# Two transformer blocks with 32 experts: expert rows gathered by products with a 0/1 matrix instead of a scatter, sorted rows and row copies

## What is computed

```
def hier_moe(h, P, l):
    t = h.reshape(-1, d)
    grp_prob = softmax(t @ P['moe_wg'][l] + P['moe_bg'][l])
    grp_gate, grp_idx = lax.top_k(grp_prob, 1)
    ...
    top_p, top_i = lax.top_k(softmax(sel), TOP_K_IN_GROUP)
    w = grp_gate * top_p / jnp.sum(top_p)
    def body(acc, xs):
        wg_e, wu_e, wd_e, cw = xs
        y = (silu(t @ wg_e) * (t @ wu_e)) @ wd_e
        return acc + cw[:, None] * y, None
```

## Time and profile before

| | us |
|---|---|
| median of three runs | 1150.37 |
| lowest and highest | 1147.16, 1150.96 |
| the profiled execution, its own time | 1151.86 |
| its span, first to last instruction | 1150.1 |
| PE busy / DVE busy / ACT busy / POOL busy | 970.8 / 487.3 / 332.5 / 138.0 |
| read from HBM | 291.87 MB |

### The profile page before, as it was taken

The page is one execution under the profiler, slowest core; times in us unless marked ns, Lnnn a source line. Parts: engine busy times, 40 slices in busy tenths (PEclk is TensorE's granted clock), DMA queues, the critical chain, the costliest instruction groups (busy, mean ns, idle before and its releaser), DMA issues.

```text
span 1150.1 us, 20717 instructions
## 1 busy us (share of the span) xinstructions
PE 970.8 (84%) x7674; PEld 646.0 (56%) x7674; DVE 487.3 (42%) x1271; ACT 332.5 (29%) x879; POOL 138.0 (12%) x193
## 2 busy tenths in 40 slices
PE   5899888999468788788879999998964887888887
PEld 3456655655345455455558888776543554555454
DVE  2079876521632333333430314685145332333334
ACT  3211353530522222221330101575132222222222
POOL 0400140000400010000010055000022100010000
PEclk8999999999679999988979999998976999999998
DMA  9999736772269999999873323100215799999993
GB/s 353 279 316 361 254 110 234 264 271 74 101 229 374 416 416 417 419 418 418 337 257 110 96 87 129 56 1 2 78 69 219 298 416 417 416 417 417 417 418 126
DMA packets 84913, 302.08 MB, mean 263 GB/s; under 512 B 5541, under 2 KB 34449, under 8 KB 68465
## 3 DMA queue, kind: packets, MB, share of 16 engines
q1 hardware_dynamic: 81584, 291.03, 65.4%
q0 software_dynamic: 2832, 8.61, 2.6%
q10 hardware_dynamic: 432, 1.57, 0.3%
HBM read 291.87 MB, written 9.32 MB: 262 GB/s over the span
## 4 chain that ended last, share of the span: by engine, by line
PE 51%; DMA 26%; DVE 14%; ACT 3%; issue 3%; SPq 1%; POOL 1%; POOLq 0%; DVEq 0%; ACTq 0%
PE banks L666 26%; DMA ring<-in_moe_w_up_dram 24%; PE banks L978 6%; PE banks L675 5%; DVE a L1508 5%; PE banks L1022 4%; PE banks L973 4%; DVE a L1443 2%; PE banks L704 2%; PE banks L1001 1%; DVE rt L1443 1%; SPq L561 1%; DMA bc<-in_moe_be_dram 1%; PE banks L949 1%; POOL bc L2041 1%
## 5 line engine op out<-in xcount | busy, mean ns | idle before, releaser
L666 PE MATMUL banks<-ring,hT 128*128 128x256 f32 (+1 forms) x720 | 153.9, 376 | 1.7 <-ACT hT L1164 1.6
L666 PEld LDWEIGHTS banks<-ring,hT 128*128 128x128 f32 x720 | 135.0, 191 | 21.3 <-DMA ring<-in_ev_w_in_dram 1.9
L1216 ACT ACTIVATE a<-banks 32x256 f32<-32x256 f32 (+1 forms) x208 | 88.3, 425 | 199.0 <-PE banks L1001 100.5
L1539 DVE SCALAR_TENSOR_TENSOR xT<-banks,mod,xT 128x128 f32<-128x128 f32 x352 | 118.7, 409 | 63.0 <-PE banks L1022 63.0
L1022 PE MATMUL banks<-a 128*128 128x384 f32 x352 | 134.0, 527 | 3.5 <-ACT a L1216 3.3
L1443 DVE TENSOR_TENSOR a<-a,banks 64x128 f32<-64x128 f32 (+1 forms) x64 | 21.7, 340 | 268.9 <-ACT a L1199 268.9
L666 PE MATMUL banks<-hT,ring 128*128 128x384 f32 x384 | 127.9, 493 | 1.6 <-ACT hT L1164 1.6
L978 PE MATMUL banks<-ring,a 128*32 128x128 f32 x2560 | 92.1, 304 | 43.1 <-DMA ring<-in_moe_w_up_dram 42.5
L978 PEld LDWEIGHTS banks<-ring,a 128*32 128x32 f32 x2560 | 80.5, 122 | 69.5 <-issue 68.4
L973 PE MATMUL banks<-ring,a 128*64 128x256 f32 x704 | 85.7, 398 | 25.5 <-DMA ring<-in_moe_w_up_dram 20.4
L666 PEld LDWEIGHTS banks<-hT,ring 128*128 128x128 f32 x384 | 73.1, 192 | 53.5 <-issue 3.8
(11 more groups left out here) (262 smaller groups left out, 1038.3 us busy)
## 6 DMA issues: line engine op xcount, KB each, us to landing
ring<-in_moe_w_gate_dram SPq DMA_DIRECT2D x64, 1024.0 KB, 8.7
ring<-in_moe_w_up_dram SPq DMA_DIRECT2D x64, 1024.0 KB, 10.8
ring<-in_moe_w_down_dram SPq DMA_DIRECT2D x64, 1024.0 KB, 10.3
ring<-in_ada_w_dram SPq DMA_DIRECT2D x44, 1024.0 KB, 8.4
ring<-in_od_w_qkv_dram SPq DMA_DIRECT2D x12, 1024.0 KB, 5.5
ring<-in_ev_w_in_dram SPq DMA_DIRECT2D x6, 1024.0 KB, 12.8
a<-sorted_rows SPq DMA_DIRECT2D x12, 512.0 KB, 6.8
a<-in_ada_w_dram SPq DMA_DIRECT2D x4, 1024.0 KB, 17.6
```

The lines of the kernel that those rows point to most:

```text
L666: mm = pe.matmul(out, lhsT, rhs, start=(k == 0), stop=(k == len(pairs) - 1))
L1216: ins = act.activation(y_pair[q % BUFFERS][row:row + rows, width * b:width * b + width], work[3][rows * b:rows * b + rows, 0:width], ACT.Copy)
L1539: ins = ve.scalar_tensor_tensor(out=xT[:, c, a:b], in0=work_banks(l)[pair + k][:, a:b], scalar=mcol(l, 5, c, j), in1=xT[:, c, a:b], op0=AL ...
```

## The change

The scatter to `sorted_rows`, the six loads, the sorted list `sortedT`, its transposes, and POOL's row copies are gone. For each tile of 128 expert rows (11 in a layer: one for the two fixed experts, ten for the groups) a 0/1 matrix `picks` of tokens by rows is made, and PE gathers the rows, already turned, by 24 products of 128x128x128 (8 chunks of features by 3 tiles of tokens, `gather`). DVE makes the `picks` of the first tile, POOL those of the other ten. The gather of a tile is done in two halves of 12 products. Half 0 is copied to `teT` by DVE, half 1 by ACT. In the loop the gather of tile q+2 lies in the first and second step of group q. The codes move behind the first expert, the store of 64 cleared rows and the wait for it go, and the loop has three bodies in place of four, with the last six steps written out.

```diff
-        for i in range(NT):
-            g.add(("codes", l, i), "s")
-        for i in range(PAIRS // P):
-            for b in range(2):
-                g.add(("sorted", l, i, b), "vs"[b])
-            if i == 0:
-                g.add(("first", l), "v")
+        g.add(("first", l), "v")
...
-                sp.wait_ge(sem("rows_sorted"), 16 * 2 * NT * (l + 1))
-                for i, rows in enumerate(sorted_in):
-                    sp.dma_start(rows, sorted_rows[P * i:P * i + P, :]).then_inc(sem(f"sorted{i}_loaded"), 16)
                 sp.wait_ge(sem("order_ready"), l + 1)
...
+                pe.wait_ge(sem("first_picked"), l + 1)
+                is_read(pe, ("htok", l, NT - 1, 1))
+                gather(opened(("rows", l, 0)), 0, 0).then_inc(sem("filled"), 1)
                 out = opened(("lead", l))
...
+                gather(opened(("rows", l, 1)), 0, 1).then_inc(sem("filled"), 1)
                 out = opened(("places", l))
...
+            def gather(out, q, half):
+
+                for c in range(4):
+                    for t in range(NT):
+                        mm = pe.matmul(out[:, P * c:P * c + P], htok[:, t, 4 * half + c:D:KD], picks[:, q % 2, t, :],
+                                       start=(t == 0), stop=(t == NT - 1))
+                return mm
...
-                    pe.wait_ge(sem("rowsT_ready"), UNROLL * t + (base + n + 1))
-                    if base + n:
+                    q, row = tile_of(n), row_in_tile(n)
+                    if q and row == 0:
+                        pe.wait_ge(sem("rows_by_vector"), UNROLL // IN_GROUP * t + (GROUPS * l + q))
+                        pe.wait_ge(sem("rows_by_scalar"), UNROLL // IN_GROUP * t + (GROUPS * l + q))
+                    if n > 1:
...
+                def gather_half(q, half, t=0):
+                    if q >= TILES:
+                        return
+                    bodies = UNROLL // IN_GROUP * t
+                    if half == 0:
+                        pe.wait_ge(sem("picked"), bodies + (GROUPS * l + q))
+                        if q > 1:
+                            pe.wait_ge(sem("rows_by_scalar"), bodies + (GROUPS * l + q - 1))
+                    else:
+                        pe.wait_ge(sem("rows_by_vector"), bodies + (GROUPS * l + q))
+                    gather(work[0], q, half).then_inc(sem("rows_gathered"), 1)
...
-                    if i:
+                    if i == 0:
+                        gather_half(q + 2, 0, t)
+                    else:
                         spread_out(q, ((0, 1), (2, 3))[i - 1], t)
+                        if i == 1:
+                            gather_half(q + 2, 1, t)
                     down(n - 1, t)
 
+                def second_step():
+                    gate_up(1)
+                    await_hid(0)
+                    hid_turn(0)
+                    gather_half(1, 0)
+                    down(0)
+                    gather_half(1, 1)
+                    pe.wait_ge(sem("diagonals_ready"), l + 1)
+                    for i in range(NT):
+                        pe.matmul(work[4 + i], ones[:, :], diagonals[:, 4 * i:4 * i + 4, :], start=True, stop=True).then_inc(sem("codes_filled"), 1)
...
+                of_the_choices(m(M_RANK), R_RANK1)
...
+                link(ve.tensor_scalar(fixed, ranks, float(ROWS), float(FURTHER_CODE), ALU.is_ge, ALU.mult))
+                link(scaled(fixed, fixed, ranks, ALU.add))
+                link(scaled(fixed, fixed, ids, ALU.add))
+                for t in range(NT):
+                    ins = ve.tensor_scalar(picks[:, 0, t, :], lane, fixed[:, t:t + 1], None, ALU.is_equal)
+                link(ins)
+                for t in range(NT):
+                    ins = ve.scalar_tensor_tensor(out=picks[:, 0, t, :], in0=lane, scalar=fixed[:, NT + t:NT + t + 1], in1=picks[:, 0, t, :],
+                                                  op0=ALU.is_equal, op1=ALU.add)
+                ins.then_inc(sem("first_picked"), 1)
...
+                scaled(pick_codes, ids.unsqueeze(1).to_broadcast((P, GROUPS, 2 * NT)),
+                       over(turn_row[:, 2:2 + 2 * GROUPS:2], 2 * NT), ALU.subtract).then_inc(sem("codes_found"), 1)
...
-                    link(pool.memset(a7[0:ROWS, 0:D], 0.0))
-                    pool.dma_start(sorted_rows[PAIRS:PAIRS + ROWS, :], a7[0:ROWS, 0:D]).then_inc(sem("pad_stored"), 16)
-                    pool.wait_ge(sem("pad_stored"), 16)
...
-                    pool.tensor_copy(teT[n % BUFFERS][:, :, 0:rows], sortedT[:, :, bass.ds(first, rows)]).then_inc(sem("rowsT_ready"), 1)
...
+                pool.wait_ge(sem("codes_found"), l + 1)
+                for q in range(1, TILES):
+                    if q == 2:
+                        is_filled(pool, ("rows", l, 1))
+                    elif q > 2:
+                        pool.wait_ge(sem("rows_gathered"), 2 * (GROUPS * l + q - 2))
+                    if GROUPS * l + q > 1:
+                        pool.wait_ge(sem("picked"), GROUPS * l + q - 1)
+                    for i in range(2 * NT):
+                        ins = pool.tensor_scalar(equal[:, i, :], lane, pick_codes[:, q - 1, i:i + 1], None, ALU.is_equal)
+                    link(ins)
+                    ins = pool.tensor_tensor(out=picks[:, q % 2, :, :], in0=equal[:, 0:NT, :], in1=equal[:, NT:2 * NT, :], op=ALU.add)
+                    ins.then_inc(sem("picked"), 1)
```

More of the change, by code:

```diff
@@ new lines, in routing @@
+                product(out[0:1, 0:NE], [(expert_values[0:NE, 0:1], at_place[0:NE, :])], True)
+                out = opened(("first", l))
+                for b in range(2):
+                    is_read(pe, ("rows", l, b))
+                w = []
+                for k in range(2):
+                    j = expert_piece(l, 0, k)
+                    pe.wait_ge(slot_sem(j), landed(j))
+                    w.append(slot(j).rearrange("p (k n) -> p k n", k=KD))
+                for c in range(KD):
+                    for k in range(2):
+                        mm = pe.matmul(out[ROWS * k:ROWS * k + ROWS, 0:FF], teT[0][:, c, 0:ROWS], w[k][:, c, :],
+                                       start=(c == 0), stop=(c == KD - 1), tile_position=(0, ROWS * k))
@@ L1222, in step @@
                     hid_copy(n - 1, t)
+                    q, i = group_step(n)
+                    if i == 1:
+                        rows_copy(q + 2, t)
                     y_copy(n - 1, t)
-                act.wait_ge(sem("cache_stored"), 32 * (l + 1))
-                for i in range(PAIRS // P):
-                    if i == 1:
-                        silu(0)
-                    is_filled(act, ("sorted", l, i, 1))
-                    done(act.activation(sortedT[:, 4:8, P * i:P * i + P], psum(("sorted", l, i, 1)).rearrange("p (c r) -> p c r", c=4), ACT.Copy))
-                load_overflow(act, l)
-                for n in range(1, STEPS_AHEAD + 1):
+                is_filled(act, ("rows", l, 1))
+                done(act.activation(teT[0][:, 4:8, :], psum(("rows", l, 1)).rearrange("p (c r) -> p c r", c=4), ACT.Copy))
+                silu(0)
+                load_overflow(act, l)
+                silu(1)
+                hid_copy(0)
+                y_copy(0)
+                rows_copy(1)
+                for i in range(NT):
+                    act.wait_ge(sem("codes_filled"), NT * l + i + 1)
+                    act.activation(pair_rows[:, 512 * i:512 * i + 512], work[4 + i], ACT.Copy).then_inc(sem("pair_rows_ready"), 1)
+                for n in range(2, STEPS_AHEAD + 1):
                     step(n)
@@ L1409, in _ @@
                     act.activation(dst, src, ACT.Exp).then_inc(sem("exp_given"), 1)
-                for i in range(NT):
-                    is_filled(act, ("codes", l, i))
-                    done(act.activation(pair_rows[:, 512 * i:512 * i + 512], psum(("codes", l, i)), ACT.Copy))
+                act.wait_ge(sem("cache_stored"), 32 * (l + 1))
                 experts(l)
@@ L1682, in routing @@
+                for t in range(NT):
+                    ins = ve.scalar_tensor_tensor(out=picks[:, 0, t, :], in0=lane, scalar=fixed[:, NT + t:NT + t + 1], in1=picks[:, 0, t, :],
+                                                  op0=ALU.is_equal, op1=ALU.add)
+                ins.then_inc(sem("first_picked"), 1)
+                count = prefix[:, 0, 16:]
                 is_filled(ve, ("counts", l))
@@ L1708, in routing @@
                 is_filled(ve, ("places", l))
-                done(ve.tensor_copy(slots[0:1, :], psum(("places", l))[0:1, 0:2 * NE]))
+                done(ve.tensor_copy(slots[0:1, :], psum(("places", l))[0:1, 0:NE]))
                 is_read(ve, ("places", l))
@@ L2099, in _ @@
-                pool.nop().then_inc(sem("rowsT_ready"), 1)
-                pool.wait_ge(sem("order_ready"), l + 1)
-                rows_copy(1)
-                with pool.Fori(0, 2 * GROUPS * IN_GROUP // (2 * UNROLL)) as t:
-                    for n in range(STATIC, STATIC + UNROLL):
-                        rows_copy(n, t)
```

(2 more changed lines are left out.)

195 lines of the change are left out of this document (79 added, 116 removed).

## The result

The changed kernel takes 1259.35 us (median of 4 runs, 1257.93 to 1260.42), the kernel before 1149.51 (4 runs, 1147.16 to 1150.96): a ratio of 1.096 (95% interval 1.093 to 1.098), slower. The forecast of 1137.7 and its range to 1150 are both missed. The profiled execution is 1259.48 us, its span 1257.6, 107.5 us over the span of before.

What follows compares the result with a forecast made beforehand. The expert stage was bound by its 96 MB of weight transfers, with PE to become the bound by 0.7 us a group. Gains of 4.5, 4.8 and 3.4 took 1150.4 to 1137.7 us, range 1127 to 1150.

Steps and rivals of the forecast that it cites:

- The gather's price: Gather products on PE: 0.120 us a record, so 2.9 us for half a tile and 5.8 for a tile.
- The bound for the step: Gather's price: 40 transposes reading with the same step of 8 elements gave 0.117 us each as a bound.
- the slow case: Each tile's 48 gather records: at 0.235 us a record, 121 us more and a time of 1259; chance 0.06.
- Slower: Rival, each tile's 48 records: 128-column weight loads not hidden, deciding from 0.132 us a record, 1259 at 0.235; chance 0.06.
- Start: Start of layer 0: gains loaded earlier, so PE's wait before the turned queries shrinks; 3.4 us gained, at most.
- Head start: Router and first experts, layer 0: expert 0 starts at 318.6 against 329.8, expert 1's products end at 326.2 against 346.4.
- Group: Three experts in the loop: PE's 17.5 us plus 5.8 of gather make 23.3, against 22.6 that the weights need.
- The last group: End of the expert stage, without a gather: 14.1 us to the end of expert 31's gate and up products.
- The allowance of 1.9 us: 19 gather halves behind expert 1's products: 0.1 us each for changes of shape and a new wait.
- Sum: Whole kernel: gains of 4.5 us in layer 0, 4.8 in layer 1 and 3.4 at the start, 12.7 together.
- The 557.1 between the layers: Layer 1: same rows taken 557.1 us after layer 0, so its stage ends at 1121.2 against 1126.0, gain 4.8.
- The tail behind expert 31 stays as it was: Work after the last expert's gate and up products: no change of time was counted.

Runs made afterwards that it cites:

- e1: Changed kernel with the four chunks of each gather half reading the stationary side at steps 8, 1, 2 and 4, giving wrong rows: 1194.37 us.
- e3: Changed kernel with ACT writing htok permuted, so the gathers read 128 neighbours, same result: 1132.62 us against 1152.14 of the kernel before, ratio 0.985.
- e6: Kernel before, its transposes of sorted rows reading neighbours instead of every eighth element: 1152.0 us against 1149.68.
- e2: Changed kernel with the gather's two operands exchanged, the 0/1 matrix stationary and the stepped token rows moving: 1255.8 us.
- e4: Kernel before, with POOL clearing and storing the 64 rows after the loads of the gains instead of ahead: 1146.32 us against 1152.14, ratio 0.9951.

## Why the prediction was wrong

**The step that failed is "The gather's price".** It took 0.120 us a record from the earlier trace rows, "the nearest in form". Those products have the gather's shape and change the stationary side each time as it does, but both of their operands lie side by side. The code of the change says `4 * half + c:D:KD`, every eighth element. Measured: 0.237 to 0.247, at either level of the clock. e1 shows it within one tile, e3 shows that nothing else slows it: with neighbours the record costs 0.115 and 0.120 in the two halves of a tile, as the forecast had it.

**The bound for the step was taken from an operation that doesn't pay it.** The prediction saw the step of 8 and priced it by the 40 transposes of the earlier trace rows, which have the same one, at 0.117. e6 shows that this row could not bound a product. The transposes differ from it in kind (one record each, where a product is two), and why they are spared is open.

**A page spoke against the change, and the prediction didn't use it.** The Trainium skill (SBUF — State Buffer, "Specifications (TRN2)") says that SBUF is read in lines of 16 bytes, that full bandwidth wants at least two hits in each, and that every crossing to a new line costs. The traces of the products agree: two elements used of 16 bytes are free (0.113 to 0.117), one doubles the record (0.242 to 0.248 at step 4). Those of the transposes don't: 0.117 at step 8. Laid beside `:D:KD` it would have made the slow case the likely one. The rule that was weighed instead, weight loads that overlap only across row groups (TensorE: Matmul & The Clock Gate, Part 3), is not borne out: in e3 all products use all rows, each loads 128 columns, and a record takes 0.115 to 0.120. Nor does that figure hold a load that fails to overlap: with the same load a record of 384 columns takes (459.40 - 456.63)/8 = 0.346, 0.115 for each 128 columns.

**The rival "Slower" had the price, 1259, and not the mechanism.** Its place (the 48 records of each tile) holds; its point of decision (0.132 us a record) was not measured, only records well on either side of it. Its 0.235 was borrowed from the lower clock, and the near agreement with 1259.35 is chance. It wasn't an unhidden load: e1 has the same loads in records of 0.113, and e2 takes the step off the loaded side and the time stays.

The rest of the working held in the main:
- **Start**: 3.5 us by the rank products (304.14 before, 300.66 after), forecast 3.4. e4 shows the same chain alone.
- **Head start**: in e3, where the gather costs what was assumed, rank comes 2.0 us earlier than before, the first half lasts 4.5 (5.0 forecast), expert 0 starts at 316.3 (318.6 - 2.0 = 316.6), and the first full group at 336.54 (335.5). Most of the missing 1.0 is the 1.48 of issue before expert 1's products, for which only the load of a register had been counted. The wait of 0.96 for POOL was forecast as 0.7 at most: its first `picks` take 5.9 us (320.43 to 326.29), where 3.7 was counted.
- **Group**: 17.2 us for the other steps where 17.5 were counted, and 22.88 in e3 against 23.3. The last group, forecast at 14.1 up to the end of expert 31's gate and up products, takes 16.4 in e3 (from 543.78), since PE waits for the ring again there (1.54 and 0.66). The allowance of 1.9 us has no counterpart in e3's groups.
- **Sum**: e3's profiled execution gains 6.4 us in layer 0 (the last gate and up products end at 560.2, 8.4 early, of which 2.0 come from the start) where 4.5 were forecast, and 6.9 in layer 1 (from the rank products to the same end) where 4.8 were. The median, 1132.6, lies inside the forecast's range, but the gain of 19.5 is 6.8 more than forecast; what the forecast had at nothing, the two closing stretches, gives 5.2 us of the profiled execution's 22.1. The 557.1 between the layers is that of the codes; expert 0 lies 556.7 later and the end of the stage 557.4, which leaves 0.3 us of the 4.8 without ground.

**"The tail behind expert 31 stays as it was" was wrong in e3**, to its good. The last 16 records of products in layer 0 (L1015, above) take 574.65 - 568.82 = 5.8 us, from the first's start to what follows. In the kernel before they take 8.46, by its timeline of PE behind layer 0:

```profile
577.21 8.53 PE L1022 MATMUL banks<-a 128*128 128x384 f32 x16 [1.64 <-ACT a L1216]
585.67 1.57 PE L728 MATMUL banks<-a,ones 128*32 128x96 f32 x48
```

So 2.6 us come from the clock: it is granted at 0.50 up to 581.5 in the kernel before and at 1.00 throughout in e3. A full PE in the loop ahead is not what decides it. Behind layer 1 the changed kernel, whose loop there has PE full at 1.00 too, takes 8.4 us:

```profile
1242.08 8.53 PE L1015 MATMUL banks<-a 128*128 128x384 f32 x16 [1.64 <-ACT a L1240]
1250.45 1.47 PE L665 MATMUL banks<-ident,xT 128*128 128x128 f32 x12
```

e4, whose PE waits in every group, takes 5.8 behind layer 0 (571.36 to 577.19), and e2 8.5 behind layer 0 and 5.7 behind layer 1. The two waits of PE just ahead of these products (1.74 and 1.64 us) are the same in all of them; why the clock is low in some is open.

## What to carry to other kernels

Before a row of the profile is taken as the price of a new product, compare how both operands are addressed, not only their shapes, and take the bound from the same kind of instruction. A float32 operand of a product, stationary or moving, should use at least two elements of every 16 bytes; if it doesn't, permute it in the copy that writes it, which cost nothing here. And where one record is issued a thousand times, run the short piece with two or three layouts before building around it: 0.117 us in one record was, by estimate, 124 us of the kernel, and the layout alone sets 1259.35 and 1132.62 us apart.

## What the runs showed of the hardware

- A product's record of 128 columns takes 0.112 to 0.120 us with steps of 1 and 2 elements, 0.163 to 0.192 with 3, 0.234 to 0.263 with 4 and 8 (one value of 0.215; stretches of 6 to 24 records). Step 2, 4 and 8 were run on either operand with the same outcome, step 3 on the stationary one alone. The slow rate doesn't follow the granted clock (0.237 to 0.246 at 1.00, 0.247 at 0.50).
- Transposes through the identity don't pay for the step: 0.117 with it, 0.114 without.
- The durations of weight loads follow the pace of the products and don't tell which operand is slow (335 ns a load in the change, 196 in e3; 5.41 us for 24 in e2, whose loads read neighbours).
- ACT's copy of 512 columns takes 0.60 us with the permuted write as without.
